# Three rotating buffers under the expert selection, and a branch product inside the attention stage

## The reference, cut to what matters

```python
def peer_ffn(h, w_q, sub_keys, expert_u, expert_v):
    q = (hb @ w_q).reshape(n, PEER_HEADS, 2, PEER_HALF_2)
    s = jnp.einsum('nhcd,hckd->nhck', q, sub_keys)
    sc, ix = lax.top_k(s, PEER_TOPK)                 # 8 heads x 2 halves, 16 of 128 keys
    cand = sc[:, :, 0, :, None] + sc[:, :, 1, None, :]
    top, pos = lax.top_k(cand.reshape(...), PEER_TOPK)
    gate = jax.nn.softmax(top, axis=-1)
    act = jax.nn.gelu(jnp.einsum('nhed,nd->nhe', expert_u[eidx], hb))
    return jnp.einsum('nhe,nhed->nd', gate * act, expert_v[eidx])

y_rw = rwkv7_time_mix(u_rw, ...)
y_mla = mla_mix(u_mla, ...)                          # 8 heads, softmax(q k^T) v
merged = gates[:, :, 0] * (y_rw @ w_br_rwkv) + gates[:, :, 1] * (y_mla @ w_br_mla)
x = x + merged @ w_out
```

## Time and profile before

| what | us |
|---|---|
| median of 3 runs | 3798.87 (3798.09 to 3800.53) |
| the profiled execution's own time | 3799.12 |
| its span, first to last instruction | 3797.4 |
| PE busy | 3336.8 (88%) |
| DVE busy | 2432.4 (64%) |
| ACT busy | 1498.4 (39%) |
| POOL busy | 426.0 (11%) |

### The profile page before, as it was taken

How to read it: one execution, slowest core, us unless ns; L and a number is a source line. 1 busy time by engine, 2 the same in 40 slices (tenths; PEclk the granted TensorE clock), 3 DMA queues, 4 the chain that set the end, 5 groups by cost and what they waited for, 6 DMA issues and landing times. The chain is left out here.

```text
span 3797.4 us, 59274 instructions
## 1 busy us (share of the span) xinstructions
PE 3336.8 (88%) x20672; PEld 2901.2 (76%) x20672; DVE 2432.4 (64%) x4939; ACT 1498.4 (39%) x2306; POOL 426.0 (11%) x460
## 2 busy tenths in 40 slices
PE   6888999999977687999999967966679799999995
PEld 5777899999874576899999963864358689999994
DVE  4689666666655589666666655553148966666663
ACT  4237444444342227444444432221223744444443
POOL 0257000000000058000000000000005800000000
PEclk8999999999988899999999988988789999999997
DMA  4411555555441320555555531001143045555552
GB/s 195 160 57 30 184 186 187 188 188 188 172 154 59 128 100 1 177 185 185 185 186 187 188 142 63 1 1 33 45 158 103 1 165 185 185 186 187 187 188 92
DMA packets 126706, 511.74 MB, mean 135 GB/s; under 512 B 14704, under 2 KB 15344, under 8 KB 119152
## 3 DMA queue, kind: packets, MB, share of 16 engines
q1 hardware_dynamic: 126576, 510.07, 37.4%
HBM read 508.96 MB, written 1.05 MB: 134 GB/s over the span
## 5 line engine op out<-in xcount | busy, mean ns | idle before, releaser
L406 PE MATMUL ps<-xh,uhigh 128*128 128x256 f32 x3072 | 871.0, 284 | 14.6 <-POOL ulow L788 14.6
L408 PE MATMUL ps<-xh,ulow 128*128 128x256 f32 x3072 | 869.8, 283 | 0.0
L407 PE MATMUL ps<-xl,uhigh 128*128 128x256 f32 x3072 | 869.7, 283 | 0.0
L406 PEld LDWEIGHTS ps<-xh,uhigh 128*128 128x128 f32 x3072 | 588.3, 192 | 32.5 <-POOL ulow L788 19.6
L407 PEld LDWEIGHTS ps<-xl,uhigh 128*128 128x128 f32 x3072 | 588.4, 192 | 12.9
L408 PEld LDWEIGHTS ps<-xh,ulow 128*128 128x128 f32 x3072 | 588.4, 192 | 0.0
L753 DVE TENSOR_TENSOR ulow<-stream,uhigh 128x1024 fp32r<-128x1024 f32 x330 | 404.4, 1225 | 201.4 <-ACT uhigh L531 201.4
L531 ACT CAST uhigh<-stream 128x1024 fp32r<-128x1024 f32 x336 | 352.7, 1050 | 433.8 <-DMA stream<-in_u 433.8
L424 PE MATMUL ps<-vhigh,chigh 128*128 128x512 f32 x1536 | 480.3, 394 | 4.7 <-DVE vlow L769 4.3
L758 DVE TENSOR_TENSOR stream<-stream,big 128x256 f32<-128x256 f32 x336 | 218.0, 649 | 404.1 <-ACT stream L589 403.9
L424 PE MATMUL ps<-vlow,chigh 128*128 128x512 f32 x1536 | 476.2, 391 | 0.0
(11 more groups left out here) (417 smaller groups left out, 4353.9 us busy)
## 6 DMA issues: line engine op xcount, KB each, us to landing
stream<-in_u SPq DMA_DIRECT2D x384, 512.0 KB, 4.2
stream<-in_v SPq DMA_DIRECT2D x369, 512.0 KB, 3.5
big<-in_wq SPq DMA_DIRECT2D x24, 1152.0 KB, 7.8
stream<-in_ab_w_in SPq DMA_DIRECT2D x4, 2048.0 KB, 11.4
stream<-in_c_w_qf SPq DMA_DIRECT2D x16, 512.0 KB, 3.6
stream<-in_c_w_ig SPq DMA_DIRECT2D x4, 2048.0 KB, 8.2
big<-in_w_gates SPq DMA_DIRECT2D x4, 2048.0 KB, 8.0
spare<-in_v SPq DMA_DIRECT2D x15, 512.0 KB, 3.4
```

The lines of the kernel that those rows point to most:

```text
L406: pe.matmul(out, uh[:, b, cols], c.xh[:, k, :], start=k == 0, stop=False)
L407: pe.matmul(out, uh[:, b, cols], c.xl[:, k, :], start=False, stop=False)
L408: ins = pe.matmul(out, ul[:, b, cols], c.xh[:, k, :], start=False, stop=k == KD - 1)
```

## The change

In `peer`, raw u tiles, `uh` and `ul` of the early tiles get a third buffer: the raw one is `spare`, the others (`uh_third`, `ul_third`) lie on the two ring buffers of the v tiles. Tile 2 is loaded ahead of the stage with tiles 0 and 1. Score tiles are dealt out anew: 0 to 3 behind the keys of round 1, 4 and 5 behind round 2, none behind round 3, and 6 to 15 behind the residual. GpSimd's picks move ahead in its list, and the low halves of tiles 16 and 17 both wait until ScalarE has made both high halves (that of 17 first). SyncE loads the first v tiles only after score tile 14, and query weight 4 ahead of the u tiles. In `mla`, attention is two heads deep, the product with `w_br_rwkv` is cut into eight halves of two matmuls that stand between the heads, its gating is done from PSUM, and the product with `w_br_mla` is gated and added tile by tile in its own stage. Both weights are loaded ahead. The separate `br_rw` and `merge` stages are gone.

```diff
@@ peer, buffers @@
+    early_u = [u[:, 0], u[:, 1], c.spare]
+    early_uh, early_ul = ([x[:, 0], x[:, 1], y] for x, y in ((uh, c.uh_third), (ul, c.ul_third)))
+    AFTER = {1: range(0, 4), 2: range(4, 6)}
@@ peer, SyncE @@
             def early(n):
-                sp.wait_ge(early_ul, n - 1)
-                sp.dma_start(u[:, n % 2], u_dram[n]).then_inc(early_landed[n % 2], 16)
+                sp.wait_ge(low_done, n - 2)
+                sp.dma_start(early_u[n % 3], u_dram[n]).then_inc(early_landed[n % 3], 16)
-            early(2)
-            early(3)
-            for n in range(3):
-                sp.dma_start(held_v[n], v_dram[n]).then_inc(held_v_landed[n], 16)
-            for h in range(SLOTS, HEADS):
-                query(h)
-            for n in range(4, HELD):
-                early(n)
-            for b in range(2):
-                sp.wait_ge(early_ul, HELD + b - 1)
-                sp.dma_start(u[:, b], u_dram[HELD + b]).then_inc(u_landed[b], 16)
+            query(SLOTS)
+            early(3)
+            early(4)
+            early(5)
+            for h in range(SLOTS + 1, HEADS):
+                query(h)
+            for n in range(6, HELD):
+                early(n)
+            for b in range(2):
+                sp.wait_ge(low_done, HELD - 2 * b)
+                sp.dma_start(u[:, b], u_dram[HELD + b]).then_inc(u_landed[b], 16)
+            sp.wait_ge(early_used, HELD - 1)
+            for n in range(3):
+                sp.dma_start(held_v[n], v_dram[n]).then_inc(held_v_landed[n], 16)
@@ peer, TensorE @@
-                for n in range(4 * r - 4, 4 * r):
+                for n in AFTER.get(r, ()):
                     early_scores(n)
...
-            for n in range(HELD - 4, HELD):
+            for n in range(6, HELD):
                 early_scores(n)
@@ peer, ScalarE @@
             def early_act(n):
...
-                if n + 2 < HELD:
-                    early_high(n + 2)
-                else:
-                    u_high(0, n + 2 - HELD, False)
+                if n + 3 < HELD:
+                    early_high(n + 3)
+                elif n + 3 == HELD:
+                    u_high(0, 1, False)
+                elif n + 1 == HELD:
+                    u_high(0, 0, False)
...
-            early_high(0)
-            early_high(1)
+            for n in range(3):
+                early_high(n)
@@ peer, GpSimd @@
-            early_low(0)
-            early_low(1)
-            for r in range(ROUNDS - 1):
-                early_low(4 * r + 2)
-                early_low(4 * r + 3)
-                pick(r)
-                early_low(4 * r + 4)
-                early_low(4 * r + 5)
-            for n in range(HELD - 2, HELD + 2):
+            for n in range(5):
+                early_low(n)
+            pick(0)
+            early_low(5)
+            early_low(6)
+            pick(1)
+            early_low(7)
+            early_low(8)
+            pick(2)
+            for n in range(9, HELD + 2):
                 early_low(n)
@@ mla @@
+    W = a.take(2 * 4 * BANK).rearrange("p (b k n) -> p b k n", b=2, k=4)
+    c.prefetch({b: [(W[:, b].rearrange("p k n -> p (k n)"), d["w_br_rwkv"][b])] for b in range(2)})
     with stage(c, "rope") as block:
...
+    c.prefetch({2 + n: [(freed[n], d["w_br_mla"][n])] for n in range(2)})
     with stage(c, "attention") as block:
...
+            def branch(x):
+                u, half = x // 2, x % 2
+                n, tt = UNITS[u]
...
+                for k in range(2 * half, 2 * half + 2):
+                    ins = pe.matmul(c.ps[:, 6 + u % 2, :], y_rw[:, k, tt * P:(tt + 1) * P], W[:, n, k, :],
+                                    start=k == 0, stop=k == 3)
+            scores(0)
+            scores(1)
+            branch(0)
+            for h in range(MLA_HEADS):
+                turn(h)
+                if h + 2 < MLA_HEADS:
+                    scores(h + 2)
+                if h:
+                    values(h - 1)
+                if h + 1 < MLA_HEADS:
+                    branch(h + 1)
+            values(MLA_HEADS - 1)
@@ mla, attention, VectorE @@
+            maxima(0)
+            maxima(1)
+            for h in range(MLA_HEADS):
+                normalise(h)
+                if h + 2 < MLA_HEADS:
+                    maxima(h + 2)
+                if h % 2 == 0 and h:
+                    branch_out(h // 2 - 1)
+            branch_out(3)
@@ mla, attention, ScalarE @@
+            exps(0)
+            exps(1)
+            for h in range(MLA_HEADS):
                 act.wait_ge(pt_ready, h + 1)
...
                 act.copy(pt[:, h % 2].rearrange("p k t -> p (k t)"), c.ps[:, 2 + h % 2, :]).then_inc(pt_moved, 1)
+                if h + 2 < MLA_HEADS:
+                    exps(h + 2)
+                if h:
+                    values_out(h - 1)
+            values_out(MLA_HEADS - 1)
+    c.prefetch(weight_loads(c, d["w_out"], 512))
@@ mla, new stage br_mla; VectorE @@
+                dve.wait_ge(done, u + 1)
...
+                dve.tensor_tensor(m2[:, u % 2], c.ps[:, u, :], c.gates[:, tt, D + n * BANK:D + (n + 1) * BANK], ALU.mult
+                                  ).then_inc(gated, 1)
+                dve.wait_ge(gated, u + 1)
+                dve.tensor_tensor(m1[:, tt, cols], m1[:, tt, cols], m2[:, u % 2], ALU.add).then_inc(moved, 1)
@@ second_block @@
-    product(c, "br_rw", d["w_br_rwkv"], 2, 512, m1, nk=4, lhs=y_rw)
-    product(c, "br_mla", d["w_br_mla"], 2, 512, m2, nk=4, lhs=y_mla)
-    c.prefetch(weight_loads(c, d["w_out"], 512))
-    chain = c.sem("merge_dve")
-    with stage(c, "merge") as block:
...
+    mla(c, d, a, y_rw, m1)
```

More of the change, by code:

```diff
@@ L782, in early_low @@
             def early_low(n):
-                done = early_ul if n < HELD else u_split
                 if n < HELD:
-                    alone(early_uh, n + 1)
-                else:
-                    alone(uh_ready, n - HELD + 1)
-                pool.tensor_tensor(ul[:, n % 2], u[:, n % 2], uh[:, n % 2].bitcast(F32), ALU.subtract).then_inc(done, 1)
+                    alone(high_done, n + 1)
+                    high, low, raw, done = early_uh[n % 3], early_ul[n % 3], early_u[n % 3], low_done
+                else:
+                    alone(uh_ready, 2)
+                    high, low, raw, done = uh[:, n - HELD], ul[:, n - HELD], u[:, n - HELD], u_split
+                pool.tensor_tensor(low, raw, high.bitcast(F32), ALU.subtract).then_inc(done, 1)
             def pick(r):
@@ L2230, in scores, with turn @@
                 ins.then_inc(s_ready, 1)
-            scores(0)
-            for h in range(MLA_HEADS):
-                if h + 1 < MLA_HEADS:
-                    scores(h + 1)
+            def turn(h):
                 pe.wait_ge(p_ready, h + 1)
@@ L2243, in _, with values @@
                 ins.then_inc(pt_ready, 1)
+            def values(h):
                 pe.wait_ge(pt_moved, h + 1)
@@ L2299, in _ @@
                 act.copy(pt[:, h % 2].rearrange("p k t -> p (k t)"), c.ps[:, 2 + h % 2, :]).then_inc(pt_moved, 1)
-                act.wait_ge(o_ready, h + 1)
-                act.copy(y[rows, h // 2, :], c.ps[rows, 4 + h % 2, 0:T]).then_inc(o_moved, 1)
-    return y, mark
+                if h + 2 < MLA_HEADS:
[4 more added lines that the diff above has]
+    c.prefetch(weight_loads(c, d["w_out"], 512))
+    m2 = a.take(2 * BANK).rearrange("p (b n) -> p b n", b=2)
+    done, moved, gated = c.sem("br_mla_done"), c.sem("br_mla_moved"), c.sem("br_mla_gated")
+    with stage(c, "br_mla") as block:
+        @block.tensor
+        def _(pe):
+            for u, (n, tt) in enumerate(UNITS):
+                if tt == 0:
+                    first_tile(c, pe, 2 + n)
+                for k in range(4):
+                    ins = pe.matmul(c.ps[:, u, :], y[:, k, tt * P:(tt + 1) * P], W2[n][:, k, :],
+                                    start=k == 0, stop=k == 3)
+                ins.then_inc(done, 1)
+        @block.vector
+        def _(dve):
+            for u, (n, tt) in enumerate(UNITS):
+                cols = slice(n * BANK, (n + 1) * BANK)
+                dve.wait_ge(done, u + 1)
+                if u >= 2:
+                    dve.wait_ge(moved, u - 1)
+                dve.tensor_tensor(m2[:, u % 2], c.ps[:, u, :], c.gates[:, tt, D + n * BANK:D + (n + 1) * BANK], ALU.mult
+                                  ).then_inc(gated, 1)
+                dve.wait_ge(gated, u + 1)
+                dve.tensor_tensor(m1[:, tt, cols], m1[:, tt, cols], m2[:, u % 2], ALU.add).then_inc(moved, 1)
 def second_block(c, d):
@@ L2387, in allocate @@
     c.sem = c.sems.open
-    c.first_landed = [nc.alloc_semaphore(name=f"first_landed{b}", num=c.sems.first + 2 * SEMS + b) for b in range(FIRST_U + 2)]
-    c.first_count = [0] * (FIRST_U + 2)
+    c.first_landed = [nc.alloc_semaphore(name=f"first_landed{b}", num=c.sems.first + 2 * SEMS + b) for b in range(FIRST_U + 3)]
+    c.first_count = [0] * (FIRST_U + 3)
     c.ahead = {}
```

84 lines of the change are left out of this document (45 added, 39 removed).

## The result

The changed kernel takes 3715.52 us (median of 4 runs, 3712.17 to 3718.13), the kernel before in the same job 3799.25 (4 runs, 3798.09 to 3800.53). The ratio is 0.9779, 95% interval 0.9762 to 0.9796. The forecast was 3719.4; the sum of its case was 79.5 us, and the medians lie 83.7 apart.

The account below looks back on a forecast made before the run. No engine is full in selection or attention, so order and waits decide. Attention to merge saves 54 us and three selections 25.5, together 79.5 off 3799.1, with the runs' median 0.25 lower: 3719.4, range 3704 to 3740.

Parts of the forecast that it names:

- the term of 2.8 for the clock: Attention: the first half of a branch product starts at the lower clock level, costing 2.8 us once.
- the 0.7 held back for a second climb: Attention to merge: 54.7 us saved, taken as 54 because a second clock climb could cost up to 2.8.
- The upper bound of 57: Attention to merge: at most 57 us saved, if no climb of the clock is paid at all.
- signs that were set down for being right: Among them: attention 36 us at a clock near 0.95; 53 to 56 us from first scores to the merge's transposes.
- rival A: Selection: VectorE-GpSimd collisions decide, five places in round 3 at 2.2 us each; layer gains 5.1, 3729.8 us; chance 0.15.
- a sign of being wrong: Selection: an index copy later than 2.2 us behind the exponential would show the forecast wrong.
- The wait goes: Selection round 2: VectorE's 4.2 us wait for GpSimd's pick vanishes, as `pick(1)` runs under the 10.2 of halves.
- the forecast's bound of 36.6: Selection: VectorE's round 3 up to the index copy takes 36.6 us if its collisions with GpSimd all stay.
- B: Attention to merge: clock stays at 1.2 GHz, 96 us for 108; gain 12, 3761.6 us; chance 0.07.
- C: Selection: the wait for the pick moves into u 17 and later rounds in full; gain 54 alone, 3745.1; chance 0.07.
- D: Expert loop: steps lock into an order where TensorE waits, 336 times; at 0.3 us a step 3820; chance 0.02.
- E: Larger gain: u 17 lands by Gelu 14, 12 a layer, and no clock climb is paid, 57: 3706; chance 0.12.

Follow-up runs that it names:

- after_again: The changed kernel run again, unedited, in the job of `split_low`, against the kernel before: 3715.25 us, ratio 0.9789.
- mla_only: Attention and branches of the change alone, selection as in the kernel before: 3735.73 us, ratio 0.9846 to the kernel before.
- picks_only: The kernel before with only GpSimd's picks moved ahead in its list; two buffers, old tile deal, old attention: 3794.89 us, ratio 0.9999.

## Why the prediction was right

The mechanisms came true, and the total is nearer than its parts: attention and the transposes behind it gave 5.1 more than the sum had, the selection 2.4 less. That these offset each other was luck.

**Attention.** TensorE needed 4.23 per head where 4.0 was taken (bounds 4.0 and 4.45): 33.8 for eight instead of 32. The groups' drains are hidden as argued, and only a little less than hoped. The end and the handover cost 1.1 (34.88 from the first scores to the product) against 1.5 and 1.1. The second product took 13.97 (forecast 13.7), and 1.84 to the transposes (2.2). Against the sum of 53.3 up to the transposes that is 1.8 more for the heads, 0.3 more for the product and 1.9 less for the ends and handovers, which cancel but for 0.2. What made 57.35 of 54 is the term of 2.8 for the clock, which was not paid, and the 0.7 held back for a second climb. The 2.8 came from a branch product that began at the lower level. But attention's first scores took 1.96 already before, and take 1.97 now; the window over them in the kernel before reads 1.00:

```profile
2663.10:2665.10 2.00, 1.96 (x8) 1.40 (x8) 0.83 (x3) 1.24 (x1) 0.00 (x0) 1.00 0.00 0
```

The stage began at full clock and lost it only in the gaps between the engines. The row that said so was among those that the sum used. (`after_again` pays 1.2, the changed kernel 0.) The upper bound of 57 allowed for it and was exceeded by 0.35, and two of the signs that were set down for being right were missed on the good side: 53 to 56 us to the transposes (50.69), and attention of 36 us at a clock near 0.95 (34.2 at 1.00).

**Not in the sum.** The merge's transposes fell from 3.65 to 1.94, because TensorE comes to them at a clock of 1.00, 1.84 behind a dense product, and not at 0.50 after 8.88 of idling. The forecast measured only up to their start. It is 1.7 us, and with it `mla_only` is accounted for.

**The selection.** Third layer, times from the first copy of queries; the forecast's are its absolute ones less 2828.05:

| step | forecast | measured |
|---|---|---|
| round 3 of VectorE starts | 77.3 | 76.8 |
| TensorE ends its last tile | 108.0 | 107.9 |
| ScalarE stands for u 17 | 5.1 | 5.45 |
| exponential starts | 111.9 | 111.9 |
| index copy starts | 113.5 | 115.6 |
| GpSimd's first keys | 116.0 to 117.2 | 116.5 |

VectorE waits for no pick, and the sum that met GpSimd in most cases (median 2406 ns) has a median of 216 ns now and a maximum of 2423. The index copy is the one step beyond its mark: the product at L718 took 2.60 against 0.42, struck by the last pair of low halves. The forecast had this only in rival A. It cost at most 1.1 us, GpSimd's wait for the index copy at L720 before its first keys: without it GpSimd would still have been held by the same pair until 2872.21. The copy came 3.71 behind the exponential in every layer; over 2.2 was set down as a sign of being wrong. That sign told true: VectorE's path had a collision that the sum left out, and half of it was hidden behind GpSimd. The first layer gained only 6.6 (8.3 in other traces of the same code): ScalarE stood 7.46 for u 17 there, where 5.1 was taken, and its exponential started at 113.9 and not 111.9; with u 17 first it starts at 110.6 in all three. The term behind it is the one that the sum took from no row: u 17 was to land 0.8 behind u 16, and in layers 1 to 3 it landed 3.21, 1.73 and 1.26 behind. Hence 23.1, not 25.5. One reading in the forecast was loose: that GpSimd sets the gate matrix's pace. Its own row has VectorE busier, 86.94 against 83.16. The two start within 0.5 us of each other behind the index copy, so the count comes out the same.

**Where the reasoning was too simple.** "The wait goes" was true, but the wait was one of several chains of equal length. Before, VectorE alone set the index copy, 8.25 behind the exponential's start. A sum over its round 3 shows how: it waited 3.84 for the pick and met GpSimd in the four places below (L692 and L636 are two instructions each, 2.36 for both unstruck).

```profile
2927.97 2.46 DVE L648 TENSOR_TENSOR big<-big 128x64 f32<-128x64 f32 x1
...
2935.68 2.40 DVE L676 TENSOR_SCALAR big<-big 128x64 uint32<-128x64 uint32 x1
...
2939.54 4.52 DVE L692 TENSOR_TENSOR big<-big,consts 128x1024 f32<-128x1024 f32 x2
2944.21 4.27 DVE L636 TENSOR_TENSOR big<-big 128x1024 f32<-128x1024 f32 x2
```

Over their unstruck lengths (0.22, 0.19, 2.36 and 2.36) that is 8.5. After, no wait, and 2.44, 1.89, 2.00 and 2.28 in place of 0.18, 0.21, 0.21 and 0.20: 7.8. So the collisions stayed, as the forecast's bound of 36.6 had it; the gain of 11.5 at VectorE's last sum (122.8 to 111.3) is 6.8 from the earlier start, 3.8 from the wait and under 1 from collisions. Of those 11.5 only 8.5 came through, since ScalarE (u 17) and GpSimd (the last pair) now stand at the same point to within 1 us. I take that meeting to be also the reason why no single part tried matters much when it is undone.

**The rivals.** A (collisions decide) had the mechanism and not the size: four places in round 3 were struck, and the softmax product with them, but the round had as many before and began 6.8 earlier. B is out by the clock of 1.00. C is out with the new list, and half alive in `picks_only`, where the wait moves as it said, into the scores instead of u 17. D is out: the loop takes 678.1. E's two halves split: its 57 came true, its early u 17 not.

The Trainium skill (SBUF — State Buffer, SBUF: two separate sides) also says which VectorE instructions can wait for GpSimd: those with two SBUF inputs, and copies, casts and single-input arithmetic in their fast modes, while a reduction never does. This case's trace agrees: a cast (L665, 1.89) and a one-input instruction (L690, 2.28) were struck as well as the sums, and none of 24 reductions of 128x1024 at L647, which took 1.20 to 1.22, though 12 of them began inside a GpSimd instruction. Counting only two-input instructions as targets, as the prediction did, misses two of the five struck in this round.

## What to carry to other kernels

When a wait is to be removed, ask which other list has the same length at that point: take the producers of the waiting engine's next two inputs, not of the next one alone. One edit to one list gave 1.1 us a layer here; the kernels with the third buffer, which loosens three lists, have all 8.5, in two other orders of the lists as well. Ask too where the shared work lands when an engine starts earlier: a wait removed can come back as collisions. Where engines take turns head by head, put two heads in flight or independent matmuls in the gaps; here either alone gave over 20 us and both together 7 to 10 more. Count the clock on both sides: the 16 transposes behind the dense stage took 1.94 at full clock, not 3.65.

## What had not been expected of the hardware

A late weight load costs more than its wait: 5.54 us of TensorE standing still were followed by a stretch at a granted clock of 0.54, which made the same 32 matmuls 16.05 instead of 13.97. The expectation had such a climb, at 2.8 us; it was 2.1, behind a shorter wait than the 7.28 of the kernel before.

A VectorE wait and a VectorE-GpSimd collision trade against each other: 3.99 us of waiting at the start of a round came back as a round 3.3 us shorter, and in `picks_only` a wait of 3.84 that was removed came back as 2.9 us more collisions.

A collision is not avoided by moving the GpSimd instruction a few us: VectorE's list at that place is nearly all targets, and moved from a 0.42 product it struck a 0.22 sum and a 2.36 pair, for 4.4 us in place of 2.2.
